# Gated-delta and mLSTM pairs that read their operands in place, and an earlier first split on GpSimd

## The reference

```python
# gated delta, per head and direction: q, k normalised, g cumulated log decay, beta a gate
L = where(strict, (k*beta) @ k.T * decay, 0);  sol = inv(I + L) @ [v*beta, k*beta*exp(g)]
o = q*exp(g) @ S + (q @ k.T * decay) @ v_new;  S = S*exp(g_last) + (k*exp(g_last-g)).T @ v_new
o = rms_norm(o_fwd + o_bwd) * silu(zgate)
# mLSTM, per head and direction: k is scaled by 64 ** -0.5
w = exp(log_w - m) * (q @ k.T);  h = (w @ v) / max(abs(sum(w)), exp(-m))
h = rms_norm(h_fwd + h_bwd) * sigmoid(o)
```

## Time and profile before

| | us |
|---|---|
| median of 3 runs (3178.83, 3178.83, 3185.92) | 3178.83 |
| span of the profiled execution | 3174.6 |
| outside the span, if that execution took the median | 4.2 |
| busy: TensorE / VectorE / ScalarE / GpSimd | 3054.9 / 2081.5 / 1657.2 / 612.3 |

### The profile page before, as it was taken

One profiled execution on the slowest core, in us unless ns is written; L12 is line 12 of the kernel. 1 busy time (PEld: TensorE's weight loads), 2 busy tenths in 40 slices (PEclk: granted clock), 3 DMA queues, 4 the chain that ended last, 5 costly groups with the idle time before them and its releaser, 6 DMA issues.

```text
span 3174.6 us, 56293 instructions
## 1 busy us (share of the span) xinstructions
PE 3054.9 (96%) x20767; PEld 2626.2 (83%) x20767; DVE 2081.5 (66%) x3474; ACT 1657.2 (52%) x2673; POOL 612.3 (19%) x517
## 2 busy tenths in 40 slices
PE   8999988899999999999999999889899999999998
PEld 7899877777888888888788998777688888888886
DVE  6775655777777777455568655567767777774554
ACT  6555654456555555444455556545465555544444
POOL 2000453440212222000000005334402221220000
PEclk9999998999999999999999999999899999999999
DMA  6666101114656666666556660021256665666664
GB/s 208 185 180 187 47 2 59 61 55 146 195 185 192 192 182 196 221 195 191 164 169 194 183 178 15 2 66 55 67 178 193 184 192 181 196 198 215 193 183 152
DMA packets 265227, 479.22 MB, mean 151 GB/s; under 512 B 17314, under 2 KB 81148, under 8 KB 264380
## 3 DMA queue, kind: packets, MB, share of 16 engines
q1 hardware_dynamic: 265020, 476.48, 49.1%
HBM read 474.32 MB, written 2.10 MB: 150 GB/s over the span
## 4 chain that ended last, share of the span: by engine, by line
PE 87%; DVE 8%; ACT 1%; issue 1%; DVEq 1%; POOL 0%; SPq 0%; DMA 0%; ACTq 0%; POOLq 0%
PE ps L643 86%; PE ps L647 1%; DVE scores L2194 1%; DVE wlo L1801 1%; DVE XS L1851 0%; ACT L1272 0%; DVE upair L1814 0%; DVE TN L1860 0%; DVE AR L2221 0%; DVE H L1833 0%; ACT XS L1272 0%; DVE st L1875 0%; DVE TN L2246 0%; DVE heads L1880 0%; POOL H L580 0%
## 5 line engine op out<-in xcount | busy, mean ns | idle before, releaser
L1801 DVE TENSOR_TENSOR wlo<-ring,whi 128x1024 fp32r<-128x1024 f32 (+4 forms) x905 | 1095.6, 1229 | 672.2 <-ACT whi L1272 666.3
L643 PE MATMUL ps<-upair,whi 128*128 128x512 f32 x4032 | 1404.4, 394 | 6.3 <-DVE upair L1814 5.7
L1272 ACT ACTIVATE whi<-ring 128x1024 fp32r<-128x1024 f32 (+4 forms) x947 | 941.0, 1002 | 795.6 <-PE ps L643 715.8
L643 PE MATMUL ps<-upair,wlo 128*128 128x256 f32 x4032 | 1121.2, 278 | 0.0
L643 PEld LDWEIGHTS ps<-upair,whi 128*128 128x128 f32 x4032 | 756.5, 188 | 182.9 <-issue 6.1
L643 PEld LDWEIGHTS ps<-upair,wlo 128*128 128x128 f32 x4032 | 758.9, 188 | 0.3 <-issue 0.2
L643 PE MATMUL ps<-whi,upair 128*128 128x390 f32 (+2 forms) x1280 | 367.5, 364 | 0.0
L625 POOL TENSOR_TENSOR YB<-YB 128x1024 f32<-128x1024 f32 x22 | 125.3, 5697 | 828.9 <-DVE YB L1824 828.9
L643 PE MATMUL ps<-whi,ghi 128*128 128x512 f32 x704 | 274.4, 390 | 0.0
L643 PE MATMUL ps<-whi,glo 128*128 128x512 f32 x704 | 274.0, 389 | 0.0
L643 PE MATMUL ps<-wlo,ghi 128*128 128x512 f32 x704 | 273.9, 389 | 0.0
(11 more groups left out here) (311 smaller groups left out, 3621.5 us busy)
## 6 DMA issues: line engine op xcount, KB each, us to landing
ring<-in_w_up_dram SPq DMA_DIRECT2D x352, 512.0 KB, 3.9
ring<-in_w_down_dram SPq DMA_DIRECT2D x176, 512.0 KB, 4.3
ring<-in_w_in_dram SPq DMA_DIRECT2D x128, 384.0 KB, 3.5
ring<-in_w_out_dram SPq DMA_DIRECT2D x64, 512.0 KB, 3.7
ring<-in_w_ple_gate_dram SPq DMA_DIRECT2D x64, 512.0 KB, 4.4
ring<-in_w_in_dram SPq DMA_DIRECT2D x51, 512.0 KB, 4.5
ring<-in_w_in_dram SPq DMA_DIRECT2D x64, 390.0 KB, 3.5
ring<-in_w_in_dram SPq DMA_DIRECT2D x32, 396.0 KB, 3.6
```

What stands on the lines that cost most here:

```text
L643: return pe.matmul(o_, a, b, start=start, stop=stop, skip_group_check=True)
L1272: return act.activation(o_, i_, f, **kw)
L1801: v.tensor_tensor(wlo[:, slot % RING, :, 0:w], ring[:, slot % RING, :, 0:w], whi[:, slot % RING, :, 0:w].bitcast(F32), SUB).then_inc(S["lo ...
```

## The change

VectorE's copies for a pair are gone. The gates are read in their places: TensorE and VectorE take column `2 * i + h` of `gates` and `mgates`. TensorE reads the values, mLSTM queries and keys, and the selector from `zgd`, `zmq` and `ident`. The factor 64 ** -0.5 moves into the product of scores and weights. The copies of the mLSTM values into `V1` move to ScalarE, behind its level 1 of the inverse. `gd_rhs` now writes its products into `gates`. The wait for `ml_expm` moves to stages 4 and 5, and TensorE's wait for `ml_in` is gone. On GpSimd the wait for `gd_ss` ahead of the first split of a pair is gone.

```diff
@@ gpsimd
                     if i:
-                        pool.wait_ge(S["gd_ss"], L * GP + i)
                         split_lo(sg, SL_OUT)
                         pool.wait_ge(S["gd_arg"], pool.snap(n * 2) + 1)
                         split_lo(sg, SL_OUT + 1)
@@ tensor
                     if stage == 1:
-                        pe.wait_ge(S["ml_in"], n + 1)
...
-   small[mh, 8 + h:9 + h].to_broadcast([MH, P]), mrow[d]
+   ident[mh, 2 * i + h:2 * i + h + 1].to_broadcast([MH, P]), mrow[d]
-   KB[0][hp, 1, j * P:(j + 1) * P], KB[0][hp, 0, :]
+   zmq[hp, i + MP, j * P:(j + 1) * P], zmq[hp, i, :]
-   gs[:, row, h:h + 1].to_broadcast([P, P])
+   pair_gates(i, row, h).to_broadcast([P, P])
-   turn(..., chg[:, h, t * P:(t + 1) * P])
+   turn(..., zgd[:, i * 2 + (2 * GH + h), t * P:(t + 1) * P])
@@ scalar
+                def ml_pair(i, n2, lv):
+                    if lv == 1:
+                        for j in range(NT):
+                            a(V1[:, j, :, 0:P], zmt[:, j, ds(i * T, T)].rearrange("p (h c) -> p h c", h=2), ACT.Copy)
@@ vector, gd_prepare
-                    v.tensor_copy(gs[:, :, :], gflat[:, :, ds(i * 2, 2)])
-                    v.tensor_copy(chg, v_)
@@ vector, ml_pair
-                    if stage == 0:
-                        v.wait_ge(S["ml_expm"], L + 1)
-                        v.tensor_copy(mgs[:, :, :], mflat[:, :, ds(i * 2, 2)])
-                        v.tensor_scalar(KB[0][:, 0, :], zmq[:, i, :], 64 ** -0.5, None, MUL)
-                        v.tensor_copy(KB[0][:, 1, :], zmq[:, i + MP, :])
-                        for j in range(NT):
-                            v.tensor_copy(V1[:, j, :, 0:P], zmt[:, j, ds(i * T, T)].rearrange("p (h c) -> p h c", h=2))
-                        v.tensor_copy(small[0:MH, 8:10], ident[0:MH, ds(i * 2, 2)]).then_inc(S["ml_in"], 1)
...
-                                last = v.tensor_tensor(w, w, ps[4 * h + 3][:, :], MUL)
+                                last = v.scalar_tensor_tensor(w, ps[4 * h + 3][:, :], 64 ** -0.5, w, MUL, MUL)
...
+                        v.wait_ge(S["ml_expm"], L + 1)
...
-   st[:, 0, 2 * h:2 * h + 2], mgs[:, 8 + 2 * d:10 + 2 * d, h], MAX
+   st[:, 0, 2 * h:2 * h + 2], mflat[:, 8 + 2 * d:10 + 2 * d, 2 * i + h], MAX
@@ vector, pair
-                        ml_pair(i, n, n2, 0)
...
-                        v.scalar_tensor_tensor(gs[:, 4 + d:8 + d:2, :], gs[:, 20 + d:24:2, :], -1.0, gs[:, 12 + d:16:2, :], MUL, MUL)\
+                        own_pair = slice(2 * i, 2 * i + 2)
+                        v.scalar_tensor_tensor(gflat[:, 4 + d:8 + d:2, own_pair], gflat[:, 20 + d:24:2, own_pair], -1.0,
+                                               gflat[:, 12 + d:16:2, own_pair], MUL, MUL)\
```

More of the change, by code:

```diff
@@ L171, in trunk @@
         gates = sb("gates", [P, 6, NT, 2 * GH])
-        gs = sb("gs", [P, 24, 2])
         gx = sb("gx", [P, 3, NT, 4 * GH])
@@ L175, in trunk @@
         mgates = sb("mgates", [P, 3, NT, 2 * MH])
-        mgs = sb("mgs", [P, 12, 2])
         place = -(-place // 128) * 128
@@ L234, in trunk @@
         ch = YB[:, 0, RW:RW + 6 * T].rearrange("p (k t) -> p k t", k=6)
-        chg = UA[:, 0:2, :]
         ewg = [UA[:, 2 + 2 * j:4 + 2 * j, :] for j in range(2)]
@@ L240, in trunk, with pair_gates, pair_mgates @@
         mrow = [cs[d][0:MH, 0:T] for d in range(2)]
+        gflat = gates[:, :, :, :].rearrange("p k t g -> p (k t g)").rearrange("p (a h) -> p a h", h=GH)
+        mflat = mgates[:, :, :, :].rearrange("p k t g -> p (k t g)").rearrange("p (a h) -> p a h", h=MH)
+        def pair_gates(i, row, h):
+            return gflat[:, row, 2 * i + h:2 * i + h + 1]
+        def pair_mgates(i, row, h):
+            return mflat[:, row, 2 * i + h:2 * i + h + 1]
         msq = mono(KB[1][:, :, :]).rearrange("p (k c) -> p k c", c=P)
@@ L267, in trunk @@
             gd_ss gd_rstd gd_done
-            ml_x ml_tanh ml_f ml_ln ml_g ml_rt ml_rows ml_back ml_backc ml_expm ml_sig ml_in ml_sc ml_mb ml_arg ml_d
+            ml_x ml_tanh ml_f ml_ln ml_g ml_rt ml_rows ml_back ml_backc ml_expm ml_sig ml_sc ml_mb ml_arg ml_d
             ml_dm ml_p ml_num ml_numc ml_ss ml_rstd ml_done
@@ L1008, in _, with ml_pair @@
                 mh = slice(0, MH)
-                def ml_pair(n, n2, stage):
+                def ml_pair(i, n, n2, stage):
                     if stage == 1:
-                        pe.wait_ge(S["ml_in"], n + 1)
                         for d in range(2):
                             for h in range(2):
-                                last = mm(ps[4 * d + 3][:, h * T:(h + 1) * T], small[mh, 8 + h:9 + h].to_broadcast([MH, P]),
+                                last = mm(ps[4 * d + 3][:, h * T:(h + 1) * T], ident[mh, 2 * i + h:2 * i + h + 1].to_broadcast([MH, P]),
                                           mrow[d], True, True)
@@ L1023, in ml_pair @@
                             for j in range(NT):
-                                last = mm(ps[4 * h + 3][:, j * T:(j + 1) * T], KB[0][hp, 1, j * P:(j + 1) * P],
-                                          KB[0][hp, 0, :], True, True)
+                                last = mm(ps[4 * h + 3][:, j * T:(j + 1) * T], zmq[hp, i + MP, j * P:(j + 1) * P],
+                                          zmq[hp, i, :], True, True)
                         last.then_inc(S["ml_sc"], 1)
@@ L1096, in decays @@
                                 row = (8 if j else 0) + 2 * t + d
-                                last = mm((ps[2 + d] if j else ps[4 * d])[:, o_], gs[:, row, h:h + 1].to_broadcast([P, P]), ident[:],
+                                last = mm((ps[2 + d] if j else ps[4 * d])[:, o_], pair_gates(i, row, h).to_broadcast([P, P]), ident[:],
                                           True, True)
@@ L1121, in _ @@
                         for t in range(NT):
-                            last = turn(ps[2][:, (2 * h + t) * P:(2 * h + t + 1) * P], chg[:, h, t * P:(t + 1) * P])
+                            last = turn(ps[2][:, (2 * h + t) * P:(2 * h + t + 1) * P],
+                                        zgd[:, i * 2 + (2 * GH + h), t * P:(t + 1) * P])
                     last.then_inc(S["gd_vt"], 1)
@@ L1135, in before_t @@
                         pe.wait_ge(S["gd_ktc"], n + 1)
-                    invert(m2, lambda d, j: scores[d][:, 2, j, :], {lv: lambda lv=lv: ml_pair(n, n2, lv) for lv in (1, 2, 4, 5)},
+                    invert(m2, lambda d, j: scores[d][:, 2, j, :], {lv: lambda lv=lv: ml_pair(i, n, n2, lv) for lv in (1, 2, 4, 5)},
                            {(0, "x", 1): lambda: out_slot(i, 1), (0, "t", 0): before_t, (2, "t", 0): lambda: out_slot(i, 2),
@@ L1639, in between_levels @@
                     def between_levels(lv):
-                        ml_pair(n2, lv)
+                        ml_pair(i, n2, lv)
                         if lv == 2:
@@ L2028, in gate_logs @@
                         v.tensor_scalar(fy, fy, -1.0, None, MUL).then_inc(S["ml_g"], 1)
-                gflat = gates[:, :, :, :].rearrange("p k t g -> p (k t g)").rearrange("p (a h) -> p a h", h=GH)
                 def gd_prepare(i):
@@ L2035, in gd_prepare @@
                         v.wait_ge(S["gd_silu"], L * 2 + 2)
-                    q_, k_, v_ = (zgd[:, ds(i * 2 + GH * j, 2), :] for j in range(3))
-                    v.tensor_copy(gs[:, :, :], gflat[:, :, ds(i * 2, 2)])
-                    v.tensor_copy(chg, v_)
+                    q_, k_ = (zgd[:, ds(i * 2 + GH * j, 2), :] for j in range(2))
                     v.tensor_tensor(KB[0][:, :, :], q_, q_, MUL)
@@ L2142, in ml_pair @@
                                     last = v.tensor_scalar(ml_flat(d)[:, h, j, :], ps[4 * d + 3][:, h * T:(h + 1) * T],
-                                                           mgs[:, 2 * d + j, h:h + 1], 0.0, SUB, MAX)
+                                                           pair_mgates(i, 2 * d + j, h), 0.0, SUB, MAX)
                             last.then_inc(S["ml_arg"], 1)
@@ L2164, in ml_pair @@
                         for h in range(2):
-                            v.tensor_tensor(st[:, 0, 2 * h:2 * h + 2], st[:, 0, 2 * h:2 * h + 2], mgs[:, 8 + 2 * d:10 + 2 * d, h], MAX)
+                            v.tensor_tensor(st[:, 0, 2 * h:2 * h + 2], st[:, 0, 2 * h:2 * h + 2], mflat[:, 8 + 2 * d:10 + 2 * d, 2 * i + h], MAX)
                         v.drain()
@@ L2194, in exponents @@
                                 last = v.tensor_scalar(scores[d][:, j, u, :], ps[2 + d if j else 4 * d][:, u * P:(u + 1) * P],
-                                                       gs[:, 8 + 2 * t + d, h:h + 1], 0.0, SUB, MIN)
+                                                       pair_gates(i, 8 + 2 * t + d, h), 0.0, SUB, MIN)
                         last.then_inc(S["gd_arg"], 1)
@@ L2259, in _ @@
                         for h in range(2):
-                            v.scalar_tensor_tensor(rf[d][:, h, :], ps[4 * d + 2][:, h * P:(h + 1) * P], gs[:, 4 + 2 * B + d, h:h + 1],
```

(3 more changed lines are left out.)

6 lines of the change are left out of this document (2 added, 4 removed).

## The result

The changed kernel took 3195.86 us (median of 11 runs, 3184.89 to 3207.93), beside 3184.86 us (11 runs, 3175.53 to 3188.98) for the kernel before. The ratio is 1.0037, with an interval of 1.0024 to 1.005: about 11 us slower. The forecast was 3174.4 us, no change that can be measured; sign and range were wrong.

A forecast was written before the change was run, and what follows sets the result against it. TensorE carries 87% of the chain, VectorE matters only at four boundaries and two pair-0 starts. Pair 0 2 x 1.3 = 2.6 plus boundaries 4 x (2.2 - 1.75) = 1.8 give 4.4: 3178.83 - 4.4 = 3174.4 us, range 3164 to 3186.

The forecast's parts named there:

- TensorE reads as many columns as before: TensorE's operand reads, listed among the parts that cost nothing.
- The early split holds the maximum: Boundary: GpSimd's earlier first split makes VectorE's two-column maximum L2165 wait, 1.75 us lost each time (ends 0 and 1.85).
- Rival 1: Boundary: the early split is harmless; 3167.4 us, or 3169.8 if only the right-hand sides are held; chance 0.13.
- L2221 gone, `decays` late next: Boundary: L2221 falls from 2.62 to about 0.41 us; exponents then wait for TensorE's decays, leaving 1.35 us.
- Stage 0's copies gone, L1880 held: Boundary: 2.9 us of copies go, but L1880 waits for GpSimd's second split and ends 2.65 us earlier.
- The mask: Boundary, stage 0: GpSimd's mask now meets L1883 rather than a copy, costing 0 to 0.69 us, taken as 0.45.
- The boundary as a whole: Passage between pairs, four in all: 2.2 us gained less 1.75 lost each, 1.8 us together.
- The clock cancels: TensorE's clock: shorter idle before the turn and longer idle before the right-hand sides were let cancel.
- rival 2: Output slot: the clock stays up at the turn, 1.8 us kept each, 7.2 more, 3167.2 us; chance 0.20.
- rivals 2 and 3: The latter: clock falls at the right-hand sides, 2.3 us each time, 9.2 in all, 3183.6 us; chance 0.17.
- Pair 0, 1.3 us each: Start of pair 0, twice: exponents start right behind mgates, 1.3 us saved each, 2.6 in all.
- Rival 4: Copies to V1 or the new product turn up on the path, at most 5.5 us, 3179.9; chance 0.03.

The follow-up runs named there:

- e2: Changed kernel with two unused pad tiles where gs and mgs were, so addresses are those of the kernel before; 3175.52 us, ratio 0.9972 to the kernel before.
- e3: Kernel before with gs and mgs allocated behind the last tile, no instruction changed; 3201.22 us, ratio 1.0045.
- e1: Changed kernel unaltered, run again beside the kernel before; 3197.52 us, ratio 1.0031.
- e7: e2 with GpSimd's splits waiting for ml_ss and gd_qk, beside VectorE operations that read PSUM; 3162.89 us, ratio 0.9949 to the kernel before.
- e11: Changed kernel with whi and wlo 128 bytes higher and all tiles behind them 512 bytes higher; 3192.51 us, one profiled run.
- e8: Changed kernel with every tile from H on, weights' parts included, 128 bytes higher; 3197.03 us, one profiled run.
- e5: e2 with GpSimd's wait for gd_ss put back, so only the copies' part of the change; 3173.56 us, ratio 0.9988 to the kernel before.

## Why the prediction was wrong, step by step

**The step that failed** is the sentence "TensorE reads as many columns as before", which priced TensorE at nothing. The count was right; the place from which the columns come was left out. The diff removes two small tiles, and that moves all that lies behind them. Its price is 2 x 5.92 = 11.8 us in the down-projections, and up to 2.9 us in the output slots. No rival contained it, since all four stood in the pairs. That it is the cause is shown from both sides: e2 takes the loss away from the changed kernel, e3 gives it to the kernel before without changing an instruction.

**What the pairs give** was too small to matter, and about as forecast.

- *The early split holds the maximum*: right, the step without a row of its own. Forecast 1.75 us, measured 1.88 - 0.23 = 1.65. The Trainium skill (SBUF — State Buffer, Who interferes with whom) says that the engine that comes first keeps the shared port for its whole length; the trace agrees, now for two columns also. Rival 1 is out.
- *L2221 gone, `decays` late next*: right. All twelve L2215 take 0.41 or 0.42 us, and the exponents wait 1.07 us for TensorE.
- *Stage 0's copies gone, L1880 held*: right. L1888 starts at 583.76 while the second split runs to 584.92 and ends at 585.47. Counted from a copy in stage 5 that both kernels have (start 553.09 before, 554.57 after), the exponents start 0.2 us later than before (forecast 0.4), L1888 ends 1.2 us earlier (forecast 0.9). The mask holds L1891 (formerly L1883) for 0.41 us (forecast 0.45): the group of two takes 1.17 instead of 0.76.
- *The boundary as a whole*: forecast 0.45 us. Measured 0.73 and 0.75 less in layer 1, but 0.58 and 0.14 more in layer 2: 0.8 us in all instead of 1.8.
- *The clock cancels*: neither right nor wrong as a sum. In layer 1 it fell at the turn, as before, so rival 2 didn't come. In layer 2 it stayed up there and fell behind the right-hand sides instead: the mechanisms of rivals 2 and 3 at once. The place isn't fixed by the kernel: in e1, the same program, the clock stayed up at the second turn of layer 1 as well. Stretches of 2 us of the changed kernel, first boundary and layer 2:

```profile
590.00:592.00 2.00, 1.47 (x7) 1.03 (x5) 1.93 (x5) 2.00 (x4) 1.53 (x4) 0.55 0.00 0
...
2144.00:2146.00 2.00, 2.00 (x12) 2.00 (x11) 1.17 (x3) 1.92 (x4) 0.00 (x0) 0.50 0.00 0
```

- *Pair 0, 1.3 us each*: right on VectorE, not at the end. The exponents start right behind `mgates`. Timeline, after (beside the earlier trace rows):

```profile
512.75 0.21 DVE L2128 COPY mgates<-ps 128x48 f32<-128x48 f32 x1 [2.47 <-PE ps L648]
512.87 2.15 DVE L2189 TENSOR_SCALAR scores<-ps,gates 128x128 f32<-128x128 f32 x8
520.42 1.06 PE L652 MATMUL ps<-ident,Z 128*128 128x128 f32 x4
```

That is 1.54 - 0.12 = 1.42 us earlier against `mgates`. But the clock comes back no earlier: the granted clock is 0.52 from 520 to 522 us and 1.00 from 522 (before, 0.53 from 518 to 520 and 1.00 from 520; the stage as a whole lies 1.9 us later). So the four turns at 520.42 now still run low. Before they took:

```profile
519.90 0.60 PE L647 MATMUL ps<-ident,UA 128*128 128x128 f32 x4
```

From the end of the RWKV stage to the first output slot 0.65 and 0.70 us are left: 1.35 instead of 2.6. With the boundaries that makes 2.1 us of the forecast 4.4.

- *Rival 4*: the copies to `V1` take 0.71 us for two on ScalarE, and 7.13 us of idle follow; the product with a factor takes 2.45 us for four, as without it (2.44). Both at nothing, as forecast. The change does what it says, and something else too.

Rivals 1 and 2 together, 2.2 + 1.8 = 4.0 us a boundary, are nearly what e7 reaches by other waits: 3.65 to 3.71.

## What to carry to other kernels

Removing or adding a tile moves the tiles behind it: before a change is judged by the engines that it touches, compare the pace of the longest stage that it doesn't touch, and give removed bytes a pad as the first experiment. A busy share of 100% says nothing of pace; the number of matmuls in a fixed stretch, or the distance of their starts, does. Where GpSimd's long two-operand work must lie beside a chain on VectorE, start it with a wait that puts it beside operations that read PSUM, not merely as early as its data allow.

## What the runs showed of the hardware

**The pace of these matmuls depends on where their two operands lie to each other.** Both operands are high or low parts, tiles declared `F32R`. 1056 products of 128 by 512 take 241.9 us when the two operands are 0 or 256 bytes apart modulo 512, 247.8 at 128 or 384, at a granted clock of 1.00 and with TensorE busy all the time. The same pairing held in the output slots (about 228.8 against 232.5 ns) and, where it was changed, in the up-projection (e11, 5.9 us a layer). The Trainium skill says that loading the next tile's weights takes no SBUF read bandwidth from the running matmul (TensorE: Matmul & The Clock Gate, Step-by-step: what each phase is for) and that TensorE never waits on anyone (SBUF — State Buffer, Who interferes with whom). Neither sentence speaks of where operands lie. Other engines were not what changed here, so the second isn't refuted; whether the weight loads and the running matmul get in each other's way at the slow distances, which would go against the first, no run here shows. The measured 2.5% stand beside both.

**The up-projection has two paces without any change.** Its matmuls follow each other every 173.5 ns on average in most layers, but every 176.6 ns in one layer of e3, e7 and e8, from beginning to end, 8.8 us longer (the layers of e11, with their other distance, at 175.6). 256 such matmuls in the input projection show two paces too, 173.6 ns in six stretches and 176.9 in eighteen, with e11's two between. Stretches of 40 us in layer 1 of the kernel before:

```profile
900.00:940.00 40.00, 40.00 (x232) 34.96 (x232) 31.22 (x40) 20.28 (x28) 10.49 (x3) 1.00 0.63 196
```

and of e7:

```profile
900.00:940.00 40.00, 40.00 (x228) 34.67 (x227) 28.05 (x40) 22.18 (x32) 5.47 (x3) 1.00 0.55 183
```

Runs of one kernel differ by 10 to 20 us, so one or two such stages would be enough for it (argued, since only profiled executions show the pace; of the 23 runs of the kernel before beside e5 to e7, 16 lie from 3175.53 to 3179.29 us and seven from 3186.75 up, none between), and a single time can't judge a change of this size. What selects the pace stays open. So does the rest of the distance between the changed kernel and e2: of 18.2 us between their spans 11.8 are the down-projections and up to 2.9 the output slots; the other 3 or 4 lie in small pieces, most of them in pairs whose clock fell at other points.
